# Two post norms done by halves, with their statistics as columns, and the convolution's norm sums placed elsewhere

## The reference

```python
# first block
x = x + rms_norm(memory_cross_attention(...), xattn_norm_post)   # "post_x"
h = rms_norm(x, ffn_norm_pre)
x = x + rms_norm(swiglu_ffn(h, w_gate_up, w_down), ffn_norm_post)  # gu0, dn0, "post_ffn"
# second block
h = x + 0.5 * swiglu_ffn_2(rms_norm_2(x, ffn1_norm[0]), ...)       # gu1, dn1
# conformer_conv: a dense layer (pw1), a gate, a causal depthwise
# convolution of 31 taps, layer_norm over the features, silu, a dense layer (pw2)
```

## Time and profile before

| | |
|---|---|
| median of 3 runs | 2889.81 us (2882.87, 2889.81, 2909.56) |
| the profiled execution | 2884.4 us, its span 2882.6 us |
| PE, DVE, ACT, POOL busy | 97%, 51%, 37%, 8% of the span |
| chain that ended last | PE 90%, DVE 5%, ACT 2%, issue 2%, POOL 1% |
| mean granted clock of TensorE | 0.978 of 2.4 GHz |

### The profile page before, as it was taken

One profiled execution on the slowest core, in us unless ns is written; L12 is line 12 of the kernel. 1 busy time (PEld: TensorE's weight loads), 2 busy tenths in 40 slices (PEclk: granted clock), 3 DMA queues, 4 the chain that ended last, 5 costly groups with the idle time before them and its releaser, 6 DMA issues.

```text
span 2882.6 us, 56396 instructions
## 1 busy us (share of the span) xinstructions
PE 2791.5 (97%) x23430; PEld 2655.6 (92%) x23430; DVE 1469.4 (51%) x1919; ACT 1075.5 (37%) x1585; POOL 244.8 (8%) x197
## 2 busy tenths in 40 slices
PE   7988998999999999999999999999999998999997
PEld 7965996999999999998789999999999985999997
DVE  6566573554424544337855443344444358544433
ACT  3247343432323323236743232224443237423221
POOL 2000200100000000005810000000000000100000
PEclk9959999999999999999989999999999999999999
DMA  5230141232232232331112223343223332232232
GB/s 188 85 103 2 67 132 37 74 103 102 89 104 87 88 102 93 96 97 67 45 49 98 102 94 94 101 137 116 95 95 95 100 131 70 74 102 94 94 94 70
DMA packets 75161, 263.96 MB, mean 92 GB/s; under 512 B 8388, under 2 KB 8516, under 8 KB 74752
## 3 DMA queue, kind: packets, MB, share of 16 engines
q1 hardware_dynamic: 69408, 248.93, 26.6%
q10 hardware_dynamic: 4608, 8.39, 0.8%
q0 software_dynamic: 992, 4.42, 0.5%
HBM read 253.29 MB, written 8.42 MB: 91 GB/s over the span
## 4 chain that ended last, share of the span: by engine, by line
PE 90%; DVE 5%; ACT 2%; issue 2%; POOL 1%; DMA 0%; SPq 0%; POOLq 0%; DVEq 0%; ACTq 0%
PE bank L465 79%; PE bank L956 2%; PE bank L559 1%; DVE w_lo L1606 1%; PE bank L516 1%; POOL c_acc L2345 1%; DVE bank L2143 1%; PE bank L1093 1%; PE bank L663 1%; PE bank L939 1%; PE bank L1081 1%; PE bank L734 1%; PE bank L749 0%; PE bank L725 0%; PE bank L1061 0%
## 5 line engine op out<-in xcount | busy, mean ns | idle before, releaser
L465 PE MATMUL bank<-h_hi,w_hi 128*128 128x256 f32 x4720 | 928.7, 278 | 1.2 <-DVE w_lo L1606 1.1
L465 PE MATMUL bank<-h_hi,w_lo 128*128 128x256 f32 x4720 | 921.4, 277 | 0.0
L465 PE MATMUL bank<-h_lo,w_hi 128*128 128x256 f32 x4720 | 921.1, 277 | 0.0
L1606 DVE TENSOR_TENSOR w_lo<-w_raw,w_hi 128x1024 fp32r<-128x1024 f32 x468 | 579.8, 1242 | 373.3 <-ACT w_hi L1127 196.0
L465 PEld LDWEIGHTS bank<-h_hi,w_hi 128*128 128x128 f32 x4720 | 713.7, 188 | 10.8 <-issue 7.1
L465 PEld LDWEIGHTS bank<-h_hi,w_lo 128*128 128x128 f32 x4720 | 712.7, 188 | 0.0
L465 PEld LDWEIGHTS bank<-h_lo,w_hi 128*128 128x128 f32 x4720 | 712.4, 188 | 0.0
L1127 ACT ACTIVATE w_hi<-w_raw 128x1024 fp32r<-128x1024 f32 x468 | 477.1, 1050 | 286.3 <-PE bank L465 175.3
L1626 DVE TENSOR_TENSOR t<-bank,rB 128x512 f32<-128x512 f32 x260 | 179.0, 690 | 510.5 <-PE bank L465 510.4
L465 PE MATMUL bank<-a_hi,w_hi 128*128 128x256 f32 x1716 | 334.1, 276 | 0.0
L465 PE MATMUL bank<-a_hi,w_lo 128*128 128x256 f32 x1716 | 334.1, 276 | 0.0
(11 more groups left out here) (315 smaller groups left out, 2641.0 us busy)
## 6 DMA issues: line engine op xcount, KB each, us to landing
w_raw<-in_w_gu SPq DMA_DIRECT2D x220, 512.0 KB, 3.3
w_raw<-in_w_dn SPq DMA_DIRECT2D x80, 512.0 KB, 3.6
w_raw<-in_w_dn SPq DMA_DIRECT2D x40, 384.0 KB, 3.1
w_raw<-in_w_pw SPq DMA_DIRECT2D x24, 512.0 KB, 3.2
w_raw<-in_w_in SPq DMA_DIRECT2D x22, 512.0 KB, 3.4
w_raw<-in_w_xkv SPq DMA_DIRECT2D x16, 512.0 KB, 3.3
...
```

The lines of the kernel that those rows point to most:

```text
L465: last = nc.tensor.matmul(dst[:, c:c + HALF], w, o[:, at + c:at + c + HALF], start=start and c == 0, stop=stop, skip_group_check=True)
L1606: V.tensor_tensor(cut(w_lo, slot, UNIT), cut(w_raw, slot, UNIT), cut(w_hi, slot, UNIT).bitcast(f32), sub).then_inc(w_lo_made, 1)
```

## The change

- Norm statistics of both seams are columns, as in `mix_factor`: `half_sum` gives 2 columns, `half_r` holds root and reciprocal, and a new `half_row` spreads them into a bank from which DVE's `post_pair` reads the factor. `pair_sums` (8 products of one column) and `gu_row` (4 of 128 columns) take the place of two `pair_sum`; ACT copies the row into `rB`.
- Where they stand on PE: `half_sum` of half 0 after 4 of the 8 chunks of the first half unit, its row after 8; those of half 1 behind the second and third pair of `dense_after_post`; `pair_sums` and `gu_row` behind the first and third unit of the last pair.
- `dense_after_post` takes chunks by pairs, and the last pair unit by unit, each giving `w_used` as it ends. The banks of the first two rounds are set by `GU_BANKS`.
- ACT and DVE do their steps of the seams in another order, and DVE's reciprocals of 256 columns are gone.
- Convolution: sum 2 moves from behind the last pw1 unit to behind taps(6), sum 4 into taps(7) after its sixth tap. Chunk 7 is shared as 14, 6, 11 instead of 12, 7, 12.

The diff, cut:

```diff
-SHARES = [(7, 11, 13)] * (KC - 2) + [(12, 7, 12)] * 2
-TAPS_PE = max(p for p, _, _ in SHARES)
+SHARES = [(7, 11, 13)] * (KC - 2) + [(12, 7, 12), (14, 6, 11)]
+DIAG0 = (0, max(p for p, _, _ in SHARES[::2]))
+DIAGS = DIAG0[1] + max(p for p, _, _ in SHARES[1::2])
...
+HALF_SUMS = {"post_x": (0, 5), "post_ffn": (5, 7)}
+HALF_ROWS = {"post_x": (0, 5), "post_ffn": (5, 5)}
+GU_BANKS = {"gu0": ((1, 2, 3, 4), (0, 5, 6, 7)), "gu1": ((0, 1, 2, 3), (4, 5, 6, 7))}
...
                                                 stop=stop and i == len(ks) - 1 and m == 2)
+                    if within and i == 3:
+                        half_sum(within, 0)
+                    if within and i == 7:
+                        half_row(within, 0)
                 return last
...
-            def pair_sum(post, half, b):
-                pe.wait_ge(x_summed, X_PAIRS[post] + 4 * half + 4)
-                for i in range(2):
-                    last = nc.tensor.matmul(bank[b][:, 0:HALF], const("ones"), sq_x[:, half * S + i * HALF:half * S + (i + 1) * HALF],
...
+            def pair_sums(post):
+                pe.wait_ge(x_summed, X_PAIRS[post] + 8)
+                for b in range(TB):
+                    for i in range(2):
+                        at = b // 2 * S + i * HALF + b % 2 * P
+                        last = nc.tensor.matmul(bank[7][:, b:b + 1], sq_x[:, at:at + P], const("one"), start=b == 0 and i == 0,
+                                                stop=i == 1, skip_group_check=True)
                 last.then_inc(stat_done, 1)
-            def half_sum(post, half, b):
+            def gu_row(name):
+                pe.wait_ge(gu_r_made, 1 + ("gu0", "gu1").index(name))
+                for b in range(TB):
+                    last = nc.tensor.matmul(bank[6][:, b * P:(b + 1) * P], gu_r[:, b:b + 1].to_broadcast([P, P]), ident,
+                                            start=b == 0, stop=b == TB - 1, skip_group_check=True)
+                last.then_inc(gu_spread, 1)
...
+            def half_sum(post, half):
                 pe.wait_ge(summed, SUM0[post] + 1 + WHOLE[post] + (half + 1) * (KC - WHOLE[post]))
-                nc.tensor.matmul(bank[b][:, 0:HALF], const("ones"), acc[:, tokens(half)], start=True, stop=True).then_inc(stat_done, 1)
+                for b in range(2):
+                    at = half * HALF + b * P
+                    last = nc.tensor.matmul(bank[HALF_SUMS[post][half]][:, b:b + 1], acc[:, at:at + P], const("one"), start=b == 0,
+                                            stop=True, skip_group_check=True)
+                last.then_inc(stat_done, 1)
+            def half_row(post, half):
+                pe.wait_ge(half_r_made, X_PAIRS[post] // 4 + half + 1)
+                for b in range(2):
+                    last = nc.tensor.matmul(bank[HALF_ROWS[post][half]][:, b * P:(b + 1) * P],
+                                            half_r(half)[:, b:b + 1].to_broadcast([P, P]), ident, start=b == 0, stop=b == 1,
+                                            skip_group_check=True)
+                last.then_inc(half_spread, 1)
...
                 q = U0[name] // 4
-                if not late:
-                    half_sum(post, 1, 5)
...
                 for half in range(2):
-                    for k in range(KC):
-                        pe.wait_ge(op_lo, R0[operand] + KC * half + k + 1)
+                    for p in range(4):
+                        pe.wait_ge(op_lo, R0[operand] + KC * half + 2 * p + 2)
                         for j in range(4):
-                            if half == 0 and k == 0:
+                            if half == 0 and p == 0:
                                 bank_free(B0[name] + j)
                                 pe.wait_ge(w_lo_made, 4 * q + j + 1)
...
+                            for k in (2 * p, 2 * p + 1):
+                                last = parts(half, j, k)
+                            if half == 1 and p == 3:
                                 last.then_inc(w_used, 1)
-                        if half == 0 and k == 0 and late:
-                            half_sum(post, 1, 5)
-                        if half == 1 and k == 1:
-                            pair_sum(post, 0, 7)
-                pair_sum(post, 1, 6)
+                                if j == 0:
+                                    pair_sums(post)
+                                if j == 2:
+                                    gu_row(name)
+                        if half == 0 and p == 1:
+                            half_sum(post, 1)
+                        if half == 0 and p == 2:
+                            half_row(post, 1)
...
-            def taps(c):
...
                 for k in range(n):
-                    at = (c % 2 * TAPS_PE + k) * P
+                    at = (DIAG0[c % 2] + k) * P
                     last = nc.tensor.matmul(bank[4 + c % 2][:], diag_w[:, at:at + P], conv_tap(c, k), start=k == 0, stop=k == n - 1)
+                    if sums is not None and k == 5:
+                        ln_sums(sums)
                 last.then_inc(c_pe, 1)
...
-                    if it == 3 and j:
+                    if it == 3 and j in (1, 2):
                         ln_sums(j - 1)
             taps(6)
+            ln_sums(2)
             ln_sums(3)
-            ln_sums(4)
-            taps(7)
+            taps(7, 4)
             for i in (5, 6, 7):
                 ln_sums(i)
...
-            def half_root(name, half, b):
+            def half_root(name, half):
                 act.wait_ge(stat_done, NORM[name] + half + 1)
-                nc.scalar.activation(rB[:, tokens(half)], bank[b][:, 0:HALF], ACT.Sqrt, scale=1.0 / D,
+                nc.scalar.activation(half_r(half), bank[HALF_SUMS[name][half]][:, 0:2], ACT.Sqrt, scale=1.0 / D,
...
             for j in range(4):
                 split("gu0", 0, 4, j)
+                if j == 3:
+                    operand_pair("post_x", 8, "ffn_norm_pre", 0, 1)
                 act.wait_ge(w_used, U0["xo"] + 4 + j + 1)
                 post_tile("post_x", bank[4 + j], yb_x, "xattn_norm_post", 4 + j, 1)
-                if j % 2:
-                    operand_pair("post_x", 8, "ffn_norm_pre", 0, j // 2)
+                if j == 1:
+                    operand_pair("post_x", 8, "ffn_norm_pre", 0, 0)
             operand_pair("post_x", 8, "ffn_norm_pre", 0, 2)
-            half_root("post_x", 1, 5)
+            half_root("post_x", 1)
             operand_pair("post_x", 8, "ffn_norm_pre", 0, 3)
...
-                half_root(name, 0, 7)
+                act.wait_ge(stat_done, NORM[name] + 1)
+                nc.scalar.activation(gu_r, bank[7][:, 0:TB], ACT.Sqrt, scale=1.0 / D, bias=const("norm_eps")).then_inc(root_done, 1)
                 split(name, 0, 4, 4)
-                half_root(name, 1, 6)
+                act.wait_ge(gu_spread, 1 + ("gu0", "gu1").index(name))
+                nc.scalar.activation(rB[:], bank[6][:], ACT.Copy).then_inc(gu_r_copied, 1)
                 split(name, 0, 4, 5)
...
-            half_root("post_ffn", 0, 0)
+            half_root("post_ffn", 0)
             split("gu1", 0, 4, 1)
+            operand_pair("post_ffn", 16, "ffn1_0", 0, 0)
             split("gu1", 0, 4, 2)
-            operand_pair("post_ffn", 16, "ffn1_0", 0, 0)
+            split("gu1", 0, 4, 3)
+            operand_pair("post_ffn", 16, "ffn1_0", 0, 1)
             act.wait_ge(w_used, UEND["dn0"])
             post_tile("post_ffn", bank[4], yb_h, "ffn_norm_post", 7, 1)
-            split("gu1", 0, 4, 3)
-            operand_pair("post_ffn", 16, "ffn1_0", 0, 1)
             operand_pair("post_ffn", 16, "ffn1_0", 0, 2)
-            half_root("post_ffn", 1, 5)
+            half_root("post_ffn", 1)
...
             def half_factor(name, half):
                 dve.wait_ge(root_done, NORM[name] + half + 1)
-                return V.reciprocal(rB[:, tokens(half)], rB[:, tokens(half)])
-            def post_pair(yb, made, half, p):
+                V.reciprocal(half_r(half), half_r(half)).then_inc(half_r_made, 1)
...
                 dve.wait_ge(*made(half, p))
+                if p == 0:
+                    dve.wait_ge(half_spread, X_PAIRS[norm] // 4 + half + 1)
                 dst = both((t0, t1)[p % 2][:])
-                r = rB[:, tokens(half)].unsqueeze(1).to_broadcast([P, 2, HALF])
+                r = bank[HALF_ROWS[norm][half]][:, 0:HALF].unsqueeze(1).to_broadcast([P, 2, HALF])
...
-                steps.done(half_factor(norm, 0))
+                half_factor(norm, 0)
                 for p in range(4):
-                    post_pair(yb, made, 0, p)
+                    post_pair(norm, yb, made, 0, p)
                     if p:
                         add_squares(norm, 0, p - 1)
+                    if p == 3:
+                        half_factor(norm, 1)
                     for u in splits[p]:
                         split(name, 0, 4, u)
                     lo_pair(name, gain, 0, p)
-                steps.done(half_factor(norm, 1))
```

(25 more changed lines are left out.)

64 lines of the change are left out of this document (34 added, 30 removed).

## The result

| | before | after |
|---|---|---|
| median, same comparison | 2893.9 us (2878.1 to 2909.6, 20 runs) | 2876.2 us (2871.0 to 2890.6, 20 runs) |
| profiled execution, span | 2884.4, 2882.6 us | 2878.0, 2876.2 us |
| mean granted clock | 0.978 | 0.981 |

The ratio is 0.9949, with an interval of 0.9931 to 0.9967: a gain of half a per cent that is clear of noise, but under 1%, so no change by the bound of the prediction. The median of 2876.2 stands 2.3 us from the forecast of 2878.5. But the medians differ by 17.7 us where 8.6 were worked out, while the two profiled executions differ by only 6.4.

The account below looks back on a forecast made before the run. TensorE, busy 97% of the span, was taken to bound the kernel. Gains of 1.9 (seam x), 3.3 (seam f) and 3.4 (convolution) make 8.6 us, from 2887.1 to 2878.5; range 2867 to 2894.

Parts of the forecast that it names:

- the bound of the prediction: Whole kernel: about 1%, 29 us, is what a measurement can tell from no change; no change was given 0.93.
- Waits of the seams: Both seams: no TensorE wait for acc, w_lo below 0.6 us each, one h_lo wait of about 0.8 in half 1.
- Seam x, 1.9 us: Cross attention output, post norm, gu0's first round: statistics and waits 5.2 us instead of 7.6, 0.5 more ahead; gain 1.9.
- The sizes of the new groups: TensorE per seam: half sums 0.9 us, half rows 0.9 plus 0.3, gu columns 1.8, gu row 1.0.
- the waits for w_lo and h_lo: Seam of post_x, gu0's first round: TensorE's remaining idle times for VectorE's lower halves were put at 1.35 us.
- The half units grew: Ahead of gu0's first round: the half units were to end 0.5 us later with the new statistics.
- Seam f, 3.3 us: Post_ffn, the same seam at the first FFN: 5.5 us instead of 9.7, minus 0.95 for later half units; gain 3.3.
- 2.4 are the clock: Seam of post_ffn: 2.4 of the 3.3 us come from the granted clock staying at 1.00 instead of falling to 0.50.
- Convolution, 3.4 us: Moved sums and chunk 7's new shares: taps(6) at full pace, 2.6 us idle before taps(7), which ends 3.4 us earlier.
- the step that took the low clock of before's taps as given: Convolution: before, taps(6) and taps(7) each spent about 6 us at the low clock.
- The sum, 8.6 us: Whole kernel: 1.9 + 3.3 + 3.4 = 8.6 us, 0.3%, for the two seams and the convolution.
- The runs before lie 27 us apart: Whole kernel: spread of the timed runs before, used beside the 1% limit of what a measurement can tell.

Follow-up runs that it names:

- Run 0: Not a follow-up run: a stretch of each trace, gu0's second round with all that follows up to dn0's half units; 322.7 us before, 322.3 after.
- after_again: The changed kernel again, unchanged, for a second trace; 2888.9 us over 12 runs, ratio 0.9967 to the kernel before.
- before_again: The kernel before again, unchanged, for a second trace; 2899.9 us in one run.
- conv_only: The kernel before with only the convolution's part of the change; 2900.2 us, ratio 0.9997.
- before_reset: The kernel before plus one 512-column float32 product ahead of each gu's long run of units; 2903.9 us, ratio 1.0020.
- before_reset2: The kernel before with three gu blocks written out instead of two and a 512-column float32 product ahead of the third; 2879.2 us, ratio 0.9942.
- early_pair_sum: The kernel before with its second pair sum moved to after the half's fourth chunk, summing the first half's squares again; 2899.3 us, ratio 1.0010.

## Why the prediction was right, and where it was not

The time and the verdict of no change were right, the sum only in part, and that 2.3 us lie between forecast and median is luck. The forecast started from 2887.1, 6.8 us below the median that before then showed, and the change gained 9.1 us more than the 8.6 worked out, mostly by a term that the prediction did not have. The two errors nearly cancel.

- **Waits of the seams.** Right. No wait for acc, w_lo at most 0.4, the clock at 1.00. h_lo waits twice 0.3 to 0.4 instead of once 0.8. Run 0 begins 27.7 us after the half units (551.61 to 579.27; 28 was said, 29.5 before). Reading the factor from a bank cost nothing: `t<-yb_x,bank` takes 682 ns. The 762 of `t<-yb_x,rB` was not cold starts but one instruction of 1.23 us among eight, the others 0.68 to 0.76.
- **Seam x, 1.9 us.** With xo at the same pace (before against after_again) it is 1.1. The sizes of the new groups were right (columns 1.70, row 0.81, half sum and half row 0.36 to 0.47). The term that was too small is the waits. It added up idle times, but a product lasts 0.28 us and the next starts after 0.11, so an idle time of 0.3 to 0.4 puts two starts 0.5 to 0.7 apart: by starts, the waits for w_lo and h_lo cost 2.0 us in after_again where 1.35 stood. The half units grew by 0.7, not 0.5, and 48 of the 192 products went at 0.118, 0.2 us in all. That a product behind a new group takes 0.20 us to the next is no loss: behind three of the four old groups it took 0.31.
- **Seam f, 3.3 us.** Measured 2.9 against the first trace of before, but 2.1 against four others. The clock fell in the old seam f in that first trace alone; in before_again, conv_only, before_reset and before_reset2 it stayed at 1.00, and the seam took 46.3 us instead of 47.0. So the term "2.4 are the clock" was worth 0.7: without the fall TensorE waits 1.2 us for h_lo (before_again). The falls do matter in another way, which the prediction did not see: the clock fell in one of the two seams in five of six traces of the old ones (four times in seam x, at 553 to 554 us) and in none of eight of the new.
- **Convolution, 3.4 us.** In the profiled pair 3.2; its mechanism came as written: taps of chunk 6 in 10.3 us, ScalarE 1.8 us idle at its fifth square, TensorE 2.6 us ahead of the last taps, these ending 3.2 us earlier against the first norm sum (at 1393.2 and 1396.4; the sum behind the taps starts at 1447.2 and 1453.6). What failed is the step that took the low clock of before's taps as given. It is there in three of six traces of the old convolution and in part in a fourth; in the other two old and new take the same time.
- **The sum, 8.6 us.** The seams of before and its variants (early_pair_sum left out) are 3.3 to 5.2 us longer than those of after_again. The old convolution is 0 to 6.4 us longer than the new one's usual 65.7, by where the clock fell, 3 in the mean of all. The lowest timed run of before in the first comparison is 2878.1 and that of after 2871.0, 7.2 apart. The rest of the 17.7 between the medians, some 10 us, is by these traces the pace, a term that the prediction did not have; a timed run leaves no trace, so for the medians this is inferred. "The runs before lie 27 us apart" stood in it as scatter; the two runs can make 12.7 and 13.4 of it. before_reset2 supports this by taking 20 us off before and leaving 13 of its 27 us of scatter. The changed kernel comes to the runs fast in all three of its traces with the new seams whole, and misses the stumble; in timed runs it was still above 2880 in 7 of 20 and 9 of 12.

Open stays what in TensorE has the two paces, what a wait does to them, why some float32 groups turn them and others do not, and why a kernel's timed runs differ between comparisons (after 2876 and 2889).
